# Modulation weights transposed: c on every partition, VectorE multiplies and sums along the free axis

## The reference

```python
c_act = jax.nn.silu(c)                       # c: (1, 1024)
for l in range(DEPTH):                       # DEPTH = 2
    mod = c_act @ w_ada[l] + b_ada[l]        # w_ada[l]: (1024, 6144)
    sh1, sc1, g1, sh2, sc2, g2 = [m[:, None, :] for m in jnp.split(mod, 6, axis=-1)]
    h = rms_norm(x, ln1_g[l]) * (1.0 + sc1) + sh1
    ...
    x = x + g1 * (merged @ w_out[l])
    h2 = rms_norm(x, ln2_g[l]) * (1.0 + sc2) + sh2
    x = x + g2 * (jnp.square(jax.nn.relu(h2 @ w_ff1[l])) @ w_ff2[l])
```

## Time and profile before

| | us |
|---|---|
| median of 3 runs (2001.36 to 2001.58) | 2001.46 |
| the profiled execution | 1998.61 |
| its span in the trace | 1997.3 |
| PE busy in the span | 1954.6 (98%) |
| DVE busy | 1385.9 (69%) |
| ACT busy | 1018.3 (51%) |
| DMA: bytes moved, mean rate | 363.23 MB, 182 GB/s |

### The profile page before, as it was taken

How to read it: one execution, slowest core, us unless ns; L and a number is a source line. 1 busy time by engine, 2 the same in 40 slices (tenths; PEclk the granted TensorE clock), 3 DMA queues, 4 the chain that set the end, 5 groups by cost and what they waited for, 6 DMA issues and landing times.

```text
span 1997.3 us, 37085 instructions
## 1 busy us (share of the span) xinstructions
PE 1954.6 (98%) x15561; PEld 1876.9 (94%) x15561; DVE 1385.9 (69%) x2291; ACT 1018.3 (51%) x1702; POOL 35.3 (2%) x56
## 2 busy tenths in 40 slices
PE   7999999999999999999999999999999999999998
PEld 7999988899999999988889999989999998899998
DVE  6776555578776677655558877677888556788854
ACT  5444455565444444445565544456555445565543
POOL 0000000000000000000000000030000003000000
PEclk9999999999999999999999999999999999999999
DMA  6775323246675577532235877343445544354553
GB/s 252 260 274 225 127 85 106 80 147 239 253 281 189 189 259 282 211 113 98 95 107 181 288 270 284 107 151 133 169 160 199 190 161 142 124 180 155 203 182 122
DMA packets 51246, 363.23 MB, mean 182 GB/s; under 512 B 6566, under 2 KB 8006, under 8 KB 9224
## 3 DMA queue, kind: packets, MB, share of 16 engines
q1 hardware_dynamic: 51080, 360.86, 51.2%
HBM read 359.78 MB, written 1.05 MB: 181 GB/s over the span
## 4 chain that ended last, share of the span: by engine, by line
PE 87%; DVE 7%; ACT 3%; DMA 2%; issue 1%; SPq 0%; DVEq 0%; ACTq 0%
PE bank L425 24%; PE bank L426 24%; PE bank L427 24%; DVE w_lo L1493 2%; PE bank L625 1%; DMA raw_a<-in_weights 1%; ACT w_hi L1028 1%; PE bank L461 1%; PE bank L457 1%; PE bank L458 1%; PE bank L517 1%; DVE full L1535 1%; PE bank L576 1%; PE bank L689 1%; PE bank L739 1%
## 5 line engine op out<-in xcount | busy, mean ns | idle before, releaser
L425 PE MATMUL bank<-xn_hi,w_hi 128*128 128x256 f32 (+1 forms) x2480 | 717.2, 289 | 5.9 <-DVE w_lo L1493 5.9
L427 PE MATMUL bank<-xn_lo,w_hi 128*128 128x256 f32 (+1 forms) x2480 | 706.8, 285 | 0.0
L426 PE MATMUL bank<-xn_hi,w_lo 128*128 128x256 f32 (+1 forms) x2480 | 705.2, 284 | 0.0
L425 PEld LDWEIGHTS bank<-xn_hi,w_hi 128*128 128x128 f32 x2480 | 466.6, 188 | 18.1 <-issue 16.1
L1493 DVE TENSOR_TENSOR w_lo<-raw_a,w_hi 128x1024 fp32r<-128x1024 f32 (+1 forms) x282 | 356.8, 1269 | 178.2 <-ACT w_hi L1028 177.4
L427 PEld LDWEIGHTS bank<-xn_lo,w_hi 128*128 128x128 f32 x2480 | 466.9, 188 | 0.1
L426 PEld LDWEIGHTS bank<-xn_hi,w_lo 128*128 128x128 f32 x2480 | 466.0, 188 | 1.1
L1493 DVE TENSOR_TENSOR w_lo<-raw_b,w_hi 128x1024 fp32r<-128x1024 f32 (+2 forms) x280 | 354.2, 1267 | 156.1 <-ACT w_hi L1028 155.2
L1028 ACT ACTIVATE w_hi<-raw_a 128x1024 fp32r<-128x1024 f32 (+1 forms) x282 | 306.3, 1088 | 242.5 <-PE bank L427 188.5
L1028 ACT ACTIVATE w_hi<-raw_b 128x1024 fp32r<-128x1024 f32 (+2 forms) x280 | 304.3, 1088 | 227.9 <-PE bank L427 195.0
L425 PE MATMUL bank<-h_hi,w_hi 128*128 128x272 f32 (+1 forms) x704 | 202.0, 287 | 0.0
(11 more groups left out here) (321 smaller groups left out, 3087.4 us busy)
## 6 DMA issues: line engine op xcount, KB each, us to landing
raw_b<-in_weights SPq DMA_DIRECT2D x123, 1024.0 KB, 4.8
raw_a<-in_weights SPq DMA_DIRECT2D x121, 1024.0 KB, 4.8
ada_raw<-in_ada_w SPq DMA_DIRECT2D x48, 1024.0 KB, 4.9
raw_a<-in_weights SPq DMA_DIRECT2D x16, 1408.0 KB, 5.8
raw_b<-in_weights SPq DMA_DIRECT2D x16, 1408.0 KB, 5.7
raw_a<-in_weights SPq DMA_DIRECT2D x2, 1152.0 KB, 5.1
raw_a<-in_weights SPq DMA_DIRECT2D x2, 640.0 KB, 4.0
cst<-in_const SPq DMA_DIRECT2D x1, 1152.0 KB, 9.2
```

The costliest lines, as they stand in the source:

```text
L425: pe.matmul(o, wh, xh, start=start, stop=False)
L426: pe.matmul(o, wl, xh, start=False, stop=False)
L427: return pe.matmul(o, wh, xl, start=False, stop=stop)
```

## The change

The modulation weights are laid out the other way round by the host: the output index lies on the partitions and the contraction index along the free axis. A piece is still 128 x 2048 fp32, 1 MB, but holds two blocks of 128 outputs with all 1024 weights of each. `c` is laid out as `c_rows`, the same 1024 values on all 128 partitions. It is loaded three times, for (0,0), (0,1) and (1,1) (the mixers overwrite it; between (0,1) and (1,0) it stays), and ACT applies SiLU to all of it in place. DVE then does a piece in two instructions `tensor_tensor_reduce`, each of which multiplies 128 x 1024 weights by `c_rows`, sums along the free axis from the bias on, and writes one column of `mod_all`. The matmuls of `reduce_modulation`, `acc`, and the bias addition are gone. Each piece is worked on later: piece 0 after step i = 1 and so on to piece 9 after i = 10, piece 10 in group g = 0 and piece 11 in g = 2 of the down product; the loads of pieces 1 to 10 move back by one step too.

```diff
@@ sync_program
-            for j in range(FG):
-                ada_after[b + 2 * j + 3] = (l, f, j)
+            ada_after[b + 3] = (l, f, 0)
+            for j in range(1, FG):
+                ada_after[b + 2 * j + 5] = (l, f, j)
             ada_after[b + 26] = (l, f, FG)
@@ load_ada
+        if j == 0 and (f or l == 0):
+            sp.dma_start(c.c_rows[:, :], arg["c_rows"]).then_inc(*k.up("c_in", (l, f), by=16))
@@ tensor_program
-    def reduce_modulation(l, f):
-        take(6)
-        pe.wait_ge(*k.at("ada_v", (l, f, FG - 1)))
-        for j in range(24):
-            if j == 20:
-                pe.wait_ge(*k.at("ada_v", (l, f, FG)))
-            m = pe.matmul(bank[6][:, j:j + 1], c.acc[:, j * P:(j + 1) * P], c.ones[:, 0:1], start=True, stop=True)
-            if j in (5, 11, 17):
-                yield
-        m.then_inc(*k.up("ada_mm", (l, f)))
@@ scalar_program, ffn
-            act.activation(c.c_act[:, :], c.vg[:, G_C:G_C + KD], ACT.Silu).then_inc(*k.up("rope_a", "c_act"))
...
+            if i == 0 and (f or l == 0):
+                act.wait_ge(*k.at("c_in", (l, f)))
+                act.activation(c.c_rows[:, :], c.c_rows[:, :], ACT.Silu).then_inc(*k.up("c_act", (l, f)))
@@ vector_program, ada_piece
-        for i in range(4):
-            w, s = c.ada_raw[:, i * 512:(i + 1) * 512], 4 * (j % 2) + i
-            if s:
-                dve.wait_ge(*k.newest("ada_v"))
-                dve.scalar_tensor_tensor(out=o, in0=w, scalar=c.c_act[:, s:s + 1], in1=o, op0=ALU.mult, op1=ALU.add).then_inc(
-                    *k.up("ada_v", (l, f, j) if i == 3 else None))
-            else:
-                dve.tensor_scalar(o, w, c.c_act[:, 0:1], None, ALU.mult).then_inc(*k.up("ada_v"))
+        for i in range(2):
+            w, n = c.ada_raw[:, i * D:(i + 1) * D], 24 * f + 2 * j + i
+            dve.tensor_tensor_reduce(out=w, in0=w, in1=c.c_rows[:, :], scale=1.0, scalar=c.bada[:, l, n:n + 1], op0=ALU.mult, op1=ALU.add,
+                                     accum_out=c.mod_all[:, l, n:n + 1]).then_inc(*k.up("ada_v", (l, f, j) if i else None))
@@ vector_program, ffn
-            ada_piece(l, f, i)
+            if i:
+                ada_piece(l, f, i - 1)
...
-                if g == 2 and s == 1:
-                    ada_piece(l, f, FG)
+                if g in (0, 2) and s == 1:
+                    ada_piece(l, f, FG - 1 + g // 2)
...
-        dve.wait_ge(*k.at("ada_mm", (l, f)))
-        half = slice(24 * f, 24 * f + 24)
-        dve.tensor_tensor(c.mod_all[:, l, half], bank[6][:, 0:24], c.bada[:, l, half], ALU.add).then_inc(*k.up("mod_v", (l, f)))
```

More of the change, by code:

```diff
@@ L211, in __init__ @@
         self.h_hi, self.h_lo = sb("h_hi", [P, KF, T], F32R), sb("h_lo", [P, KF, T], F32R)
-        self.acc, self.ada_raw = sb("acc", [P, ADA_N // 2]), sb("ada_raw", [P, 2048])
+        self.c_rows, self.ada_raw = sb("c_rows", [P, D]), sb("ada_raw", [P, 2 * D])
         ffn_end = place
@@ L343, in load_ada @@
             sp.wait_ge(*k.at("x_hi", ("ffn", l, f, KD - 1)))
-        at = (f * 12 + j) * 2048
-        sp.dma_start(c.ada_raw[:, :], arg["ada_w"][l, :, at:at + 2048]).then_inc(*k.up("ada_in", (l, f, j), by=16))
+        if j == 0 and (f or l == 0):
+            sp.dma_start(c.c_rows[:, :], arg["c_rows"]).then_inc(*k.up("c_in", (l, f), by=16))
+        at = (f * 12 + j) * 2 * D
+        sp.dma_start(c.ada_raw[:, :], arg["ada_w"][l, :, at:at + 2 * D]).then_inc(*k.up("ada_in", (l, f, j), by=16))
     def load_vectors1(l):
@@ L533, in ffn @@
         for g in range(4):
-            chain = reduce_modulation(l, f) if g == 3 else iter(())
             for half in range(2):
@@ L548, in ffn @@
                         free[b] = [("tile_v", ("dn", l, f, 2 * g + j))]
-                    next(chain, None)
                     u += 1
@@ L1585, in gains @@
     def gains(l):
+        dve.wait_ge(*k.at("ada_v", (l, 1, FG)))
         for i, (g, sc) in enumerate(((V_LN1, 8), (V_LN2, 32))):
@@ L1644, in ffn @@
                 u += 1
-            ada_piece(l, f, i)
+            if (l, f, i) == (0, 0, 0):
+                dve.wait_ge(*k.at("first_in", "all"))
+                dve.wait_ge(*k.at("table_in", "all"))
+            if i:
+                ada_piece(l, f, i - 1)
         if (l, f) == (0, 0):
-            dve.wait_ge(*k.at("first_in", "all"))
-            dve.wait_ge(*k.at("table_in", "all"))
             rope_angles()
@@ L2147, in _layout @@
         np.concatenate([i["q_norm"][l]] * 2)[:, None], np.concatenate([i["k_norm"][l]] * 2)[:, None]], axis=1) for l in range(L)])
-    f["vecg"] = np.concatenate([_columns(i["final_norm"]), _columns(i["final_g_2"]), _columns(i["c_2"][0])], axis=1)
-    a = i["w_ada_2"].reshape(L, 2, 4, P, 2, 6, 512).transpose(0, 3, 4, 5, 1, 2, 6)
-    f["ada_w"] = a.reshape(L, P, 24 * 2048)
+    f["vecg"] = np.concatenate([_columns(i["final_norm"]), _columns(i["final_g_2"])], axis=1)
+    f["ada_w"] = i["w_ada_2"].reshape(L, D, ADA_N // P, P).transpose(0, 3, 2, 1).reshape(L, P, ADA_N // P * D)
+    f["c_rows"] = np.broadcast_to(i["c_2"][0], (P, D))
     f["b_ada"] = np.stack([_columns(i["b_ada_2"][l]) for l in range(L)])
@@ L2177, in _layer2 @@
     return ws, np.stack(vs)
-_NAMES = ["x0", "weights", "w2cat", "lr_w", "vec1", "vec2", "vecg", "ada_w", "b_ada", "pos", "const", "masks"]
+_NAMES = ["x0", "weights", "w2cat", "lr_w", "vec1", "vec2", "vecg", "ada_w", "c_rows", "b_ada", "pos", "const", "masks"]
 def kernel(**inputs):
```

17 lines of the change are left out of this document (6 added, 11 removed).

## The result

| | before | after |
|---|---|---|
| median of the runs, us | 2001.41 (1994.83 to 2001.58, 4 runs) | 1972.97 (1971.86 to 1975.68, 4 runs) |
| ratio, 95% interval | | 0.9868 (0.9845 to 0.989) |
| the profiled execution, us | 1998.61 | 1971.86 |
| its span, us | 1997.3 | 1970.6 |

The change gains 28 us by the medians and 26.8 us between the two profiled executions, where the prediction had 20.6.

A forecast was written before the change was run, and what follows sets the result against it. PE was taken as the bound in the feed-forward stages. Inner bursts 16.2 us plus stage-end bursts 4.4 us gave 20.6 us, other terms nothing: 1980.9 us from a median of 2001.46, range 1976 to 1988.

The forecast's parts named there:

- Removed from PE: In the feed-forward stages, dropping 16 bursts of partition-sum matmuls at 1.35 us each, less at stage ends, gains 20.6 us.
- DVE's new instruction: On DVE a piece of the modulation takes 2.86 us against 2.87 before, so its load is unchanged and stays hidden.
- Rival (a): On DVE the accumulating form runs at half rate, a piece taking 5.00 us: 1981 to 1983 us; chance 0.08.
- Moved: Pieces done a step later on DVE, one of them in g = 0 of the down product, gain or cost nothing.
- Added: Three loads of c_rows on SP's queue and a SiLU on ACT cost nothing, at most 2.7 us in three stages.
- The clock: PE's half-speed stretch after (1,1) costs 1.7 us again; two such stretches more or fewer give 3.4 us either way.
- The range: Whole kernel 1976 to 1988 us: best 21.6 us gained and 3.4 of slow clock saved; worst adds 3.4, 2.7 and 1.
- (b): PE's time was not the bound at the bursts; it would wait for w_lo, losing half the gain: 1991 us; chance 0.03.
- (d): The removed passes on PE lay beside main matmuls, so removal brings nothing: 2001 us; chance 0.02.
- (c): DVE becomes the bound; gain eaten at 6.18 us a piece, 2040 us at three cycles an element; chance 0.05.

## Why the prediction was right or wrong

**Removed from PE: right.** 16 bursts of 1.35 us were expected, less 0.22 at three ends and 0.32 at the fourth. The end of (0,0) after the change, for the earlier trace rows:

```profile
220.85 0.29 PE L460 MATMUL bank<-xn_hi,w_hi 128*128 128x272 f32 x1
...
222.58 0.70 PE L510 MATMUL bank<-sumsq,cst 128*128 128x272 f32 x2
...
221.99 0.44 DVE L1598 TENSOR_TENSOR sumsq<-sumsq,sq 128x272 f32<-128x272 f32 x1 [0.50 <-ACT sq L1033]
...
223.32 0.49 ACT L1020 ACTIVATE rstd<-bank,cst 128x272 f32<-128x272 f32 x1 [0.94 <-PE bank L510]
```

The last unit ends where L460 starts. From there to the norm's matmul it is 222.58 - 220.85 = 1.73 us; in the earlier trace rows it is 228.11 - 225.26 = 2.85 from the burst's start. The norm gained 1.12 us, against 1.13 predicted, and the next limit is the one named: `sumsq` ends at 222.43 and L510 follows 0.15 later. ACT's wait fell from 2.00 to 0.94. In all 20.05 us for 20.6.

**DVE's new instruction: right in what it decides, 13% too dear.** A row takes 1280 ns (predicted 1285) and its write-out 83 (predicted 145, from the `COPY`). But the rows of the pair start 1.20 us apart and overlap, so a piece takes 2.48 and not 2.86. It costs nothing since it is hidden, as predicted. Rival (a) fell: (1280 - 217)/1024 = 1.04 ns an element, the rate of the rows without a sum. The halving that the Trainium skill states (Vector Engine (DVE) Microarchitecture Reference, Points that are easy to get wrong) is not seen here: `scalar_tensor_tensor` with two fp32 sources ran at 1.043 ns an element without a sum and the new instruction at 1.04 with one. The trace calls the new one CUSTOM_DVE_ANT_0, so whether it has the shape that the page names is not shown.

**Moved: "Nothing" for the piece in g = 0 was wrong in its reason, at a small price.** It counted DVE's work per unit and not who waits for it in what order. The residual update stands behind the piece and has one unit of time, and the room there was 0, not 1.6 us. It cost some 0.3 to 0.6 us here, and 26.6 with the work doubled, half-clock stretches included. The prediction also held that the piece's load keeps its place relative to the DVE work; here the load itself is late (DVE waits 3.3 us for `ada_raw` in three places, each at g = 0).

**Added: right.** `c_rows` and the SiLU cost nothing: the lead is constant to 0.05 us through the first steps of (0,1) and (1,1).

**The clock:** two half-clock stretches either way were allowed; the profiled pair shows a little more of it around 1293, 0.8 us.

**The range: here the forecast failed.** "At best 21.6 us and two slow-clock stretches fewer" took the sums' removal as the best case, and so held the pace of every other matmul as unchanged, without a reason given. That term was put at nothing and measured 6.8 us: f lies at another address and its 1536 matmuls came every 113.35 ns instead of 117.78. No row ahead of the result shows that address, but the change's own lines do: they shorten a vector ahead of f. Half-clock stretches, for which the range had allowed, did not bring the time below it. The prediction also let nothing of the change reach the second network; 1.3 us came at the norm of `cq` there, behind a load of weights that landed sooner. With it the small gains and losses of the table about cancel. Without f's move, 26.8 - 6.8 = 20.0 us would have been left, an estimate of 2001.4 - 20.0 = 1981.4 us, for 1980.9 predicted and inside the range. The 1981.19 measured with f moved back lies closer than it should: there the kernel before took 1997.63, and the gain was 17 us (13 to 21).

**The rivals.** (b) and (d) are excluded by the 20.05 us that the bursts gave back. (c) is excluded at one piece a step; with the work tripled DVE is the bound.

## What to carry to other kernels

Price a removed instruction on the bounding engine by the distance of starts around it, which held here to 3%. When work is moved on a hidden engine, don't count its load in that stretch but look for the instruction that now stands behind it and for who waits for that, and how long. A change of the memory layout, even one of 128 bytes by a dropped vector, is a change of PE's pace of its own and belongs in the range.

## What the runs showed of the hardware that was not expected

The distance between matmuls with their own weights, on an engine that is never idle and at full clock, depends on where the moving rows start. At 256 columns: 113.35 ns at 64 bytes past a multiple of 256, 117.78 at 192, 118.67 at 0, 119.99 at 128; at 272 columns 123.3 at 64, 125.35 at 128 and 126.7 at 0. All these kernels have the weights at place 128, so the distance between rows and weights may be what counts. At place 64 and 256 columns there are two paces, 113.3 and 117.8 ns. A stretch without a pause keeps the one it has, for up to 1.5 thousand matmuls, and the changes that were looked at stand at a pause. In the kernel with all rows at 64, the first rows of `xn` in the feed-forward ran at 113.5 up to a pause at 1425.7, the rest at 117.8 behind it, and f went on so. The kernel before shows it too: its rows of `y` in the second network, at place 64, run at 113.3 until PE waits for DVE at 1431.49, and at 117.8 from there. In seven traces with f at 64 behind rows of `xn` that change places, f had the fast pace in both layers each time. What in the chip makes the two paces, and what chooses between them in (1,1), was not settled. The Trainium skill (TensorE: Matmul & The Clock Gate, section Back-to-back issue gap) gives N/2.4 + 2.5 for the gap of an isolated matmul, an estimate of 109.2 ns at 256 columns; the rows here, a stream with weight loads of their own, lie 4 to 11 ns above it.
